# Norms of cached keys made in a gather stage of the layer before, and an odd layer reordered around its recurrence

## The reference

```python
def mla_expand(ckv, w_uk, w_uv, g_kn):
    k_nope = rms_norm((ckv @ w_uk).reshape(ckv.shape[:-1] + (D_HEADS, D_NOPE)), g_kn)
    v = (ckv @ w_uv).reshape(ckv.shape[:-1] + (D_HEADS, D_VDIM))
    return k_nope, v

def odd_sample(...):
    u, q_nope, q_pe, ckv, kpe = odd_heads(h, pos, w_in, g_cq, g_ckv, w_uq, g_qn, g_qr, g_kr)
    oc, s_re, s_im = s5_scan(u, s0_re, s0_im, *s5p)
    def one(args):
        pages, qn, qp, cn, kn = args
        c_all = jnp.concatenate([pool_ckv[pages].reshape(-1, D_KV_LORA), cn], axis=0)[None]
        k_all = jnp.concatenate([pool_kpe[pages].reshape(-1, D_ROPE), kn], axis=0)[None]
        k_nope, v = mla_expand(c_all, w_uk, w_uv, g_kn)
        return mla_core(qn[None], qp[None], k_nope, k_all, v, pos)[0]
```

## Time and profile before

| what | value |
| --- | --- |
| median of 3 runs (lowest to highest) | 2556.54 us (2550.62 to 2556.87) |
| the profiled execution's own time | 2558.51 us |
| its span | 2556.8 us |
| PE / DVE / ACT / POOL busy | 2106.9 / 1198.0 / 633.0 / 943.8 us |
| first gather stage | about 811 to 1252 us of the span |
| odd layer up to its output projection | about 1253 to 1566 us |
| mean granted TensorE clock over the span | 0.91 |

### The profile page before, as it was taken

The page is one execution under the profiler, slowest core; times in us unless marked ns, Lnnn a source line. Parts: engine busy times, 40 slices in busy tenths (PEclk is TensorE's granted clock), DMA queues, the critical chain, the costliest instruction groups (busy, mean ns, idle before and its releaser), DMA issues.

```text
span 2556.8 us, 37396 instructions
## 1 busy us (share of the span) xinstructions
PE 2106.9 (82%) x13993; PEld 1531.5 (60%) x13993; DVE 1198.0 (47%) x3472; ACT 633.0 (25%) x959; POOL 943.8 (37%) x844
## 2 busy tenths in 40 slices
PE   8887899999998666666678788999999996666666
PEld 3653589999996323333346235799999983323322
DVE  2442279713333433575257942699233333333332
ACT  1421115455552000000024341144555540000000
POOL 0001017870003655666203130059720016656564
PEclk9898999999999888888788898999999998888887
DMA  5425314444446999999701131434444459999998
GB/s 215 175 85 207 127 72 157 154 161 165 166 165 238 350 340 324 337 339 341 285 4 43 54 124 33 140 108 157 165 161 166 165 183 326 336 329 343 334 346 300
DMA packets 164885, 525.38 MB, mean 205 GB/s; under 512 B 20930, under 2 KB 37090, under 8 KB 164194
## 3 DMA queue, kind: packets, MB, share of 16 engines
q0 software_dynamic: 88064, 311.21, 34.2%
q1 hardware_dynamic: 76642, 211.79, 23.9%
HBM read 520.23 MB, written 2.69 MB: 205 GB/s over the span
## 4 chain that ended last, share of the span: by engine, by line
PE 59%; DMA 17%; POOL 9%; DVE 7%; issue 5%; ACT 2%; another core or an unknown queue 0%; SPq 0%; DVEq 0%; ACTq 0%; POOLq 0%; PEldq 0%
DMA v_slot<-in_peer_v,v_rows 15%; PE bank L636 15%; PE bank L788 10%; PE bank L790 9%; PE bank L789 9%; PE bank L847 8%; POOL v_slot L586 6%; POOL u_low L575 3%; PE bank L1099 1%; PE bank L842 1%; DVE s_turned L1519 1%; PE bank L662 1%; PE bank L656 1%; DVE s_tmp L2074 1%; DMA region<-in_cache_a_kt 1%
## 5 line engine op out<-in xcount | busy, mean ns | idle before, releaser
L586 POOL DMA_INDIRECT v_slot<-in_peer_v,v_rows x576 | 546.8, 949 | 790.3 <-PE bank L790 441.1
L788 PE MATMUL bank<-h_parts,u_high 128*128 128x288 f32 x2048 | 606.7, 296 | 6.3 <-POOL u_low L575 5.7
L789 PE MATMUL bank<-h_parts,u_high 128*128 128x288 f32 x2048 | 604.4, 295 | 0.0
L790 PE MATMUL bank<-h_parts,u_low 128*128 128x288 f32 x2048 | 602.7, 294 | 0.0
L847 PE MATMUL bank<-v_slot,weight_columns 128*32 128x512 f32 x2048 | 335.9, 785 | 278.2 <-DMA v_slot<-in_peer_v,v_rows 253.5
L575 POOL TENSOR_TENSOR u_low<-u_slot,u_high 128x1024 fp32r<-128x1024 f32 x120 | 320.8, 2683 | 370.3 <-ACT u_high L1290 370.3
L788 PEld LDWEIGHTS bank<-h_parts,u_high 128*128 128x128 f32 x2048 | 384.1, 188 | 9.6 <-POOL u_low L575 9.1
L790 PEld LDWEIGHTS bank<-h_parts,u_low 128*128 128x128 f32 x2048 | 385.8, 188 | 0.0
L789 PEld LDWEIGHTS bank<-h_parts,u_high 128*128 128x128 f32 x2048 | 384.6, 188 | 0.0
L1290 ACT CAST u_high<-u_slot 128x1024 fp32r<-128x1024 f32 x256 | 268.8, 1050 | 399.9 <-PE bank L790 245.8
L847 PEld LDWEIGHTS bank<-v_slot,weight_columns 128*32 128x32 f32 x2048 | 72.9, 127 | 405.3 <-issue 330.5
(11 more groups left out here) (341 smaller groups left out, 2167.8 us busy)
## 6 DMA issues: line engine op xcount, KB each, us to landing
u_slot<-in_peer_ut SPq DMA_DIRECT2D x256, 512.0 KB, 3.4
w_q<-in_peer_w_q SPq DMA_DIRECT2D x8, 2048.0 KB, 16.6
v_slot<-in_peer_v,v_rows POOLq DMA_INDIRECT x576
region<-in_ev_w_in SPq DMA_DIRECT2D x4, 2048.0 KB, 15.4
region<-in_cache_a_kt SPq DMA_DIRECT2D x8, 960.0 KB, 12.7
region<-in_cache_a_v SPq DMA_DIRECT2D x8, 960.0 KB, 14.8
region<-in_pool_kv POOLq DMA_DIRECT2D x32, 128.0 KB, 3.2
region<-in_pool_kv SPq DMA_DIRECT2D x32, 128.0 KB, 5.4
```

The lines of the kernel that those rows point to most:

```text
L586: pool.indirect_dma_start(out=VS[n % NVS], out_offset=None, in_=v_rows, in_offset=bass.IndirectOffsetOnAxis(ap=IDX[:, t:t + 1], axis=0)).t ...
L788: pe.matmul(bank, uh, HR[:, 0, c, :], start=(c == 0), stop=False)
L789: pe.matmul(bank, uh, HR[:, 1, c, :], start=False, stop=False)
L790: ins = pe.matmul(bank, ul, HR[:, 0, c, :], start=False, stop=(c == KC - 1))
```

## The change

All norms of cached keys leave the odd layer. They are made in the gather stage of layer 0, passes 45 to 68 (`NORMS_AT`), in four blocks of six passes. TensorE has three places in a pass (behind spread, pick and values); at each of them `key_norms(q, third)` issues the sum for the previous square and the next projection, 16 of each in a block, so that place 17 of the 18 has only a sum and the last nothing. Projections go to bank 6 and sums to bank 7, which are tile 0's and free by then. A sum now stands alone, where before four of them ran side by side. ScalarE squares each projection, DVE takes variances and reciprocals in its passes. The latents are loaded for this by SP into two buffers of their own (`CKN`), 64 page loads more than before; the first 32 are asked for in pass 40. They are loaded once more in the odd layer, for the scores.

In the odd layer DVE now begins with the absorbed queries, the states of the samples and the scores of half 0, and then goes through the four quarters with half 1's scores before the fourth. TensorE begins with half 0's scores. The gate's matmuls (`W_GLU`) run column chunk by column chunk as the quarters finish. The value pages of samples 0 and 1 are loaded earlier; the queues' lists are reordered to match.

```diff
+NORMS_AT, NORMS_N = 45, 64
@@ SP, in layer 0's gather stage
                     load(BBD, I["s5_b"], "s5_b_loaded")
+                    load(W_UKN, I["mla_w_uk"], "s5_b_loaded")
+                    sp.wait_ge(sem("picked_full"), NS // 4 + 32)
+                    for k in range(4):
+                        if k >= 2:
+                            sp.wait_ge(sem("keys_projected"), 16 * (k - 1))
+                        for i in range(4):
+                            pages_of(sp, CKN[k % 2][:, i], I["pool_ckv"][:, :, 0:P], 4 * (k // 2) + i, f"norm_pages_loaded{k % 2}", 4 * (k % 2), 4)
                     sp.wait_ge(sem("s5_factors_made"), 3)
+                    sp.wait_ge(sem("keys_projected"), NORMS_N)
...
@@ GpSimd, odd layer
-                pool.wait_ge(sem("quarter_ready"), 2)
-                for b in (6, 7):
-                    pages_of(pool, CKPT[b], I["pool_ckv"][:, :, 0:P], b, "latents_loaded_by_pool1")
                 pool.wait_ge(sem("sd_scores"), 1)
                 for b in (2, 3):
                     pages_of(pool, CKPV[b], I["pool_ckv"][:, :, P:2 * P], b, "values_loaded_by_pool0")
                 for b in (6, 7):
                     pages_of(pool, KPP0[DR * (b - 4):DR * (b - 3)], I["pool_kpe"], b, "kpp_loaded_by_pool1")
-                pool.wait_ge(sem("y_ready"), 4)
+                pool.wait_ge(sem("quarter_ready"), 2)
+                for b in (6, 7):
+                    pages_of(pool, CKPT[b], I["pool_ckv"][:, :, 0:P], b, "latents_loaded_by_pool1")
+                pool.wait_ge(sem("y_ready"), 3)
                 for b in (6, 7):
                     pages_of(pool, CKPV[b], I["pool_ckv"][:, :, P:2 * P], b, "values_loaded_by_pool1")
@@ TensorE, gather stage
+                def key_projection(n):
+                    k, m, i = n // 16, n % 16 // 4, n % 4
+                    if n == 0:
+                        pe.wait_ge(sem("x_tile_updated"), 6 * l + 5)
+                        pe.wait_ge(sem("s5_b_loaded"), 32)
+                    if n % 16 == 0:
+                        pe.wait_ge(sem(f"norm_pages_loaded{k % 2}"), 256 * (k // 2 + 1))
+                    if n >= 1:
+                        pe.wait_ge(sem("key_squares"), n)
+                    pe.matmul(banks[6][:, :], W_UKN[:, m * P:m * P + P], CKN[k % 2][:, i].rearrange("p j n -> p (j n)"),
+                              start=True, stop=True).then_inc(sem("keys_projected"), 1)
+                def key_sum(n):
+                    k, m, i = n // 16, n % 16 // 4, n % 4
+                    if n % 16 == 0 and k >= 1:
+                        pe.wait_ge(sem("key_vars"), k)
+                    pe.wait_ge(sem("key_squares"), n + 1)
+                    pe.matmul(banks[7][32 * i:32 * i + 32, :], SUMW[:, m, :], KSQ[n % 4], start=(m == 0), stop=(m == 3),
+                              skip_group_check=True).then_inc(sem("key_squares_used"), 1)
+                def key_norms(q, third):
+                    k, at = (q - NORMS_AT) // 6, 3 * ((q - NORMS_AT) % 6) + third
+                    if l == 0 and 0 <= k < 4:
+                        if 1 <= at <= 16:
+                            key_sum(16 * k + at - 1)
+                        if at < 16:
+                            key_projection(16 * k + at)
...
                     if q < NGR:
                         spread_i1(q)
+                    key_norms(q, 0)
                     if 1 <= q <= NGR:
                         pick(q - 1)
+                    key_norms(q, 1)
                     if q >= 2:
                         values(q - 2)
+                    key_norms(q, 2)
@@ DVE, gather stage
+                    at = q - NORMS_AT - 6
+                    if l == 0 and at in (0, 6, 12, 18):
+                        key_vars(at // 6)
...
+                        if at >= 0 and at % 6 in (1, 2):
+                            key_scales(at // 6, at % 6 - 1)
@@ TensorE, odd layer
-                key_norms(0, 0)
+                latent_scores(0)
+                sample_states_out()
+                latent_turn(0)
+                latent_values(0)
                 states_out(0)
                 states_in(3)
-                key_norms(0, 1)
+                latent_out_turn(0)
                 states_out(1)
-                sample_states_out()
-                latent_scores(0)
-                key_norms(1, 0)
-                latent_turn(0)
-                states_out(2)
-                latent_values(0)
-                states_out(3)
-                key_norms(1, 1)
-                latent_out_turn(0)
                 latent_scores(1)
-                pe.wait_ge(sem("zg_ready"), 4)
...
                 latent_turn(1)
                 latent_values(1)
+                states_out(2)
                 latent_out_turn(1)
+                states_out(3)
+                glu = [to_act() for _ in range(4)]
+                for c in range(4):
+                    pe.wait_ge(sem("zg_ready"), c + 1)
...
@@ DVE, odd layer
+                absorbed_queries()
+                sample_states()
+                dve.wait_ge(sem("tbldn_loaded"), 16)
+                latent_scores(0)
+                out_of_sample_states()
                 states_turn(0)
                 states_scan(0)
                 states_turn_back(0)
-                absorbed_queries()
                 states_turn(1)
+                latent_out(0)
+                out_of_states(0)
                 states_scan(1)
                 states_turn_back(1)
-                key_vars(0, 0)
...
```

More of the change, by code:

```diff
@@ L280, in build @@
         SQL = lat.take("latent_squares", 416)
[L281 to L284 removed]
+        BSC_TMP = tile_at("s5_b_tmp", [2, SCH, 32], HB[0] + 8192)
+        after = Row(lat.at - 416 - 2 * NT + (PAGES + 1) * P, HB[0] + 8192)
+        TBLD = after.take("mla_mask", 384)
+        RK = [tile_at(f"key_scale{r}", [PAST], at) for r, at in enumerate((HB[0] + 8192, HB[1] + 8192))]
+        KSQ = [tile_at(f"key_squared{n}", [512], HB[3] + 512 * n) for n in range(2)]
+        KSQ += [tile_at(f"key_squared{2 + n}", [512], HB[3] + 3072 + 512 * n) for n in range(2)]
+        CKN = [tile_at(f"ckv_t_norm{n}", [4, 4, P], at) for n, at in enumerate((HB[2] + 2048, HB[3] + 1024))]
+        W_UKN = tile_at("w_uk_norm", [512], HB[3] + 8576)
+        SUMW = tile_at("sum_columns", [4, DH * DEC_T], HB[3] + 9088)
         heads = Row(HB[1] + 4096, HB[2])
@@ L1369, in _, with key_square, key_root @@
             act.activation(S5P[:, 9, :], S5P[:, 5, :], ACT.Sin).then_inc(sem("s5_mag"), 1)
+            def key_square(n):
+                act.wait_ge(sem("keys_projected"), n + 1)
+                if n >= 4:
+                    act.wait_ge(sem("key_squares_used"), n - 3)
+                act.activation(KSQ[n % 4], banks[6][:, :], ACT.Square).then_inc(sem("key_squares"), 1)
+            def key_root(k):
+                act.wait_ge(sem("key_vars"), k + 1)
+                half = RK[k // 2][:, 512 * (k % 2):512 * (k % 2) + 512]
+                act.activation(half, half, ACT.Sqrt).then_inc(sem("key_roots"), 1)
+            if live(3):
+                for n in range(NORMS_N):
+                    if n >= 16 and n % 16 == 8:
+                        key_root(n // 16 - 1)
+                    key_square(n)
+                key_root(3)
+                act.wait_ge(sem("key_squares_used"), NORMS_N)
             def odd():
@@ L1664, in s5_angles, with sum_columns, key_vars, key_scales @@
                 say("s5_factors_made")
+            def sum_columns():
+                link(dve.memset(SUMW, 0.0))
+                for h in range(DH):
+                    step(dve.memset(SUMW[HD * (h % 2):HD * (h % 2) + HD, h // 2, DEC_T * h:DEC_T * h + DEC_T], 1.0))
+                settle()
+            def key_vars(k):
+                dve.wait_ge(sem("key_squares_used"), 16 * k + 16)
+                TS(RK[k // 2][:, 512 * (k % 2):512 * (k % 2) + 512], banks[7][:, :], 1.0 / DN, EPS, ALU.mult, ALU.add)
+                say("key_vars")
+            def key_scales(k, part):
+                if part == 0:
+                    dve.wait_ge(sem("key_roots"), k + 1)
+                at = 512 * (k % 2) + 256 * part
+                scales = RK[k // 2][:, at:at + 256]
+                link(dve.reciprocal(scales, scales))
             def s5_factors():
@@ L2039, in odd @@
                     say("qk_ready")
-                link(dve.memset(SUMW, 0.0))
-                for h in range(DH):
-                    step(dve.memset(SUMW[HD * (h % 2):HD * (h % 2) + HD, h // 2, DEC_T * h:DEC_T * h + DEC_T], 1.0))
-                settle()
                 TS(CBD[:, 1], CBD[:, 1], -1.0, None, ALU.mult)
@@ L2099, in sample_states @@
                     say("samples_ready")
-                def key_vars(r, c):
-                    bank = full()
-                    TS(RK[:, r, 512 * c:512 * c + 512], bank[:, :], 1.0 / DN, EPS, ALU.mult, ALU.add)
-                    free()
-                    if c == 1:
-                        say("key_vars")
-                def key_scales(r):
```

(2 more changed lines are left out.)

110 lines of the change are left out of this document (29 added, 81 removed).

## The result

The changed kernel takes 2595.8 us (median of 4, 2591.5 to 2598.8) where the kernel before takes 2556.5: a ratio of 1.0151, 95% interval 1.0129 to 1.0173. It is 39 us slower. Run again later on another chip, beside other kernels, the ratio was 1.0174 (1.0143 to 1.0205).

What follows compares the result with a forecast made beforehand. The gathers were taken to bound the gather stage. Stage +58 - 4.5 + 6 = +59.5 and odd layer -29 made +30 on 2556.5, so 2586.5 us; range 2554 to 2608, likeliest case's own 2570 to 2604.

Steps and rivals of the forecast that it cites:

- TensorE becomes the bound: Gather stage: with the norms TensorE, not the gathers, sets the pace, 8.6 us a pass against 6.16.
- Rival 2: Gather stage stays gather-bound, norms slip into TensorE's idle time: 2536 us; chance 0.14 together with rival 3.
- Rival 3: Gather stage at its lower bound (+33), odd layer free of queues (-50): 2538 us; chance 0.14 together with rival 2.
- Rival 4: Handshake and drains dear (+73 to +80), pages late, odd layer gives only 20: 2619 us; chance 0.08.
- A block is 51.6 us, +58 in all: Gather stage, six passes on TensorE: own work 18.8, projections 14.5, sums 14.8, handshakes 3.5 us; four blocks add 58.
- A lone sum is as dear as a full matmul: Gather stage: a 32-column sum standing alone costs 0.92 us; sixteen cost 14.8, where four times four cost 4.2.
- The drain at a change of mode, sum +73: Gather stage: if each tiling mode change costs 0.15 us, the 64 sums pay 19 us and the total is +73.
- The bounds of the stage: Gather stage: +33 with no handshake (7.5 us a pass), +80 if every sum waits 0.84 us.
- rivals 1 and 3: Rival 1: slower as summed, 2586 us, chance 0.70. Rival 3: stage at lower bound, odd layer free of queues, 2538.
- Page loads +6: Gather stage: second load of 64 pages, 12.4 us of queue rate, 6 us exposed, between 0 and 16.
- The tail gives 4.5 back: End of the gather stage: gathers landed early make the last five groups take 27 us, not 31.5.
- The odd layer gives 29: Odd layer: norms gone, three waits on page queues walked through, projection starts at 1537 not 1566; bounds 18 to 50.

Runs made afterwards that it cites:

- the experiment: Second load of the 64 pages given back to the changed kernel stripped of norms, with projections as empty steps: 0.9936 of the kernel before.
- no norms: Changed kernel without the cached keys' norms and second page load, key scales set to one: 0.9919 of the kernel before.
- Sharing the queues: Changed kernel with SyncE issuing 16 of the first 32 rotary key pages and 8 of GpSimd's 16 value pages: 1.0102 of the kernel before.
- the other order: Changed kernel with the step waiting for sample values put behind its quarter's turn back, on TensorE and VectorE: 1.0096 of the kernel before.
- sums twice: Changed kernel with each of the 64 lone sums issued twice in a row on the same columns: 1.0416 of the kernel before.
- sums in fours: Changed kernel with sums issued four at a time, each on its own 32 columns: 0.9975 of the kernel before.
- the kernel of seven passes: Changed kernel with sums four at a time, shared page loads, late values, and each block spread over seven passes: 0.9898 of the kernel before.

## Why the prediction was right, point by point

The time came out 9 us above the 2586 named and inside both ranges; the terms hold to different degrees.

- *TensorE becomes the bound of 24 passes.* Right, as the window and the waits show. Rival 2 (the norms slip into idle time) fell: it needed a pair of 1.13 us and a pair costs 1.96. Rival 3 fell on both halves, with 8.8 us a pass and not 7.5, and 26.5 us from the odd layer and not 50. Rival 4 fell too: the pages were not late, and the odd layer gave more than 20.
- *A block is 51.6 us, +58 in all.* Measured 211.8 / 4 = 53.0, +64. This term was mis-sized by 6 us, but that is not where the 9 us went: the pages (3.7 too dear) and the end of the stage (1.2 more given back) made up for most of it, and the whole stage came out within 1 us of +59.5. That closeness is luck. Own work was right (3.13 against 3.14). Projections cost 0.99 on average and sums 0.97, not 0.91 and 0.92: 16 x 0.08 + 16 x 0.05, some 2.1 us a block, which is what the mode changes add; the stall was 0.46 and not 0.7, 5 x 0.24 = 1.2 less; and a wait I had left out, the last block's variance on DVE ahead of the first sum (3.2 us in two waits), adds 0.8.
- *A lone sum is as dear as a full matmul.* Right, and the point on which the sign hung. The doubled sums give 0.88 us for one that changes nothing. Four side by side cost one.
- *The drain at a change of mode, sum +73.* That sum took 0.15 us a change; measured are 0.06 to 0.1. The rule of the Trainium skill (TensorEngine Tiling (Array Packing), Key Properties) holds in kind; its +73 is 9 over the 64 measured, my +58 is 6 under.
- *The bounds of the stage.* Their arithmetic does not hold. Without any handshake the terms themselves make 8.0 us a pass and +45, not 7.5 and +33; with 0.84 at every one of the 64 sums they make +98, not +80. Likewise halfway between rivals 1 and 3 lies 2562, not 2558. The measured +64 lies inside either pair of bounds.
- *Page loads +6.* By the profiles the values' start before the norms came 264.4 us into the stage against 262.1 before, +2.3, where the kernels below range from 256.6 to 264.9 with and without these loads; the experiment finds nothing beyond its error. Too dear by about that much, inside its bounds of 0 to 16, and wrong in reason.
- *The tail gives 4.5 back.* 28.6 us for five groups against 31.5: 3.0, and 2.7 more before the odd stretch, for which I have no cause.
- *The odd layer gives 29.* 26.5, twice over (no norms: 26.4). The walk through the queues named each of the three waits: rotary keys 6.5 us named, 7.8 measured; first values 2 named, 4.4 measured; second 8 named, 8.7 measured. Together they were 4.4 us longer than named, and 2.5 of these are missing in the sum. Sharing the queues took 12 us away and the other order 12 more. One step came out by luck: the gate was to take some 10 us and hide well under the load of the weights. From the end of quarter 4 to the projection's last other input it took 14.5 us (1593.15 to 1607.65), and ended only 0.4 us before the weights, so both set the start.
- What is left open: the stage of before itself was 575.0 us in its profile and 567.9 in the kernel that has the same work there, on another chip. So the price of the norms is 60 to 66 us, and which of the two holds for the first chip, the runs don't settle; nor do they tell whether the 8 us before the stage were chance alone. No run takes the norms out of the old order of the odd layer, so how the 26.5 us divide between the missing norms and the new order is not shown.

## What to carry to other kernels

Idle time of an engine is room only for work cheaper than the idle time: price the added instruction in the form it will have there, alone, not in the company it had before. A narrow matmul cost here as much as a full one of the same moving columns, so move such matmuls in packs that fill the array, not one by one. And when work is spread into a loop with a fixed order, check on each engine what stands behind every new wait: here two reciprocals placed two passes too early cost some 18 us, 12.9 of them plain waiting, and pages issued one after another by one engine 12.

## What the runs showed of the hardware

- One float32 matmul of 128 x 512 on 32 columns of the array takes 0.88 us at the full clock ahead of another on the same columns (sums twice), 0.95 to 0.98 ahead of a full one; four on different columns take 1.00 together (sums in fours). A change between 32-column and full matmuls adds 0.06 to 0.1 us.
- With 4.2 MB of page loads from SyncE's queue beside GpSimd's gathers the total rose from 341 to 364 GB/s and the gathers moved 61.1 MB in 180 us against 61.3. The gathers alone, at a DMA share of 0.94, were not at the limit.
- TensorE's granted clock in the gather stage was 0.83 to 0.88 where it waited for rows a third of the time, and 1.00 where the norms filled it. The values then took 1.9 us each time, where some had taken 2.8 to 3.6.
- ScalarE loads a table for 1.28 us at the first square root of the norms. In the stage of norms it is the only one: the squares after that root and the three later roots (at 1188.93 us and on in the kernel of seven passes) take none.
- When TensorE had waited 5.3 us in the kernel of seven passes, its next matmuls ran at the lower clock: a pick of 2.08 us for 1.11. The mean granted clock from 1141.40 to 1149.50 us was 0.70, and from 1150 to 1190 it was 1.00.
